# A decoder step on one core: latent attention over the cache four sequences at a time, and inter-chunk matmuls in alternating head parity

## The reference, cut to what matters

```
num = einsum('bhts,bshv->bthv', w, v) + einsum('bht,bthk,bhkv->bthv', e_inter, q, C)
```

```
s = (einsum('bthc,bsc->bhts', ql, ckv) + einsum('bthr,bsr->bhts', qr, krope)) * SOFTMAX_SCALE
s = where(k_pos[None, :] <= qp[:, None], s, -inf)
p = softmax(s, axis=-1)
o = einsum('bhts,bsc->bthc', p, ckv)
```

## Time and profile before

| what | us |
|---|---|
| median of three runs | 2011.48 (2008.69 to 2012.48) |
| profiled execution | 2009.03 |
| its span | 2007.4 |
| PE busy | 1830.7 |
| DVE busy | 1213.2 |
| ACT busy | 925.8 |
| inter-chunk matmuls, first to DVE's copy | 152.94 to 174.73 |
| sample attention, first transpose to `uv` | 732.84 to 893.67 |
| `uv` and `wo` | 893.67 to 935.4 |
| first MoE matmul | 981.59 |

### The profile page before, as it was taken

How to read it: one execution, slowest core, us unless ns; L and a number is a source line. 1 busy time by engine, 2 the same in 40 slices (tenths; PEclk the granted TensorE clock), 3 DMA queues, 4 the chain that set the end, 5 groups by cost and what they waited for, 6 DMA issues and landing times.

```text
span 2007.4 us, 23398 instructions
## 1 busy us (share of the span) xinstructions
PE 1830.7 (91%) x8410; PEld 1404.4 (70%) x8410; DVE 1213.2 (60%) x1250; ACT 925.8 (46%) x808; POOL 92.0 (5%) x155
## 2 busy tenths in 40 slices
PE   5999979999979878888799999999999999999994
PEld 4746657999954553347587787877878778787783
DVE  2102684444344332223488888888888888888886
ACT  1100022443211111102477777777777677777774
POOL 2100020001001002200100000000000000000001
PEclk9995559999989568898799999999999999999997
DMA  9910042434724002202399999999999999999993
GB/s 275 366 44 1 0 48 89 165 100 130 223 87 171 10 0 62 70 14 105 135 368 370 357 369 338 388 359 359 370 338 386 358 360 369 341 380 353 371 366 138
DMA packets 219023, 458.37 MB, mean 228 GB/s; under 512 B 11189, under 2 KB 45562, under 8 KB 218762
## 3 DMA queue, kind: packets, MB, share of 16 engines
q1 hardware_dynamic: 209034, 428.96, 59.7%
q0 software_dynamic: 8656, 28.13, 5.0%
q10 hardware_dynamic: 1280, 0.54, 0.2%
HBM read 447.11 MB, written 17.30 MB: 231 GB/s over the span
## 4 chain that ended last, share of the span: by engine, by line
PE 83%; DVE 7%; ACT 5%; issue 2%; DMA 2%; POOL 0%; SPq 0%; ACTq 0%; POOLq 0%; DVEq 0%
PE bank L388 15%; PE bank L390 15%; PE bank L389 15%; PE bank L384 8%; ACT wpart L1580 3%; PE wide L390 2%; PE wide L388 2%; PE wide L389 2%; PE bank L759 2%; DVE wpart L916 2%; PE bank L568 2%; PE wide L742 2%; PE bank L800 2%; PE bank L703 1%; PE wide L397 1%
## 5 line engine op out<-in xcount | busy, mean ns | idle before, releaser
L916 DVE TENSOR_TENSOR wpart<-mring,wpart 128x2048 fp32r<-128x2048 f32 x339 | 775.5, 2290 | 159.3 <-ACT wpart L1580 158.4
L1580 ACT ACTIVATE wpart<-mring 128x2048 fp32r<-128x2048 f32 x336 | 643.0, 1917 | 202.3 <-PE bank L390 109.1
L388 PE MATMUL bank<-wpart,xgp 128*128 128x512 f32 x896 | 360.5, 402 | 7.5 <-DVE wpart L916 5.3
L390 PE MATMUL bank<-wpart,xgp 128*128 128x512 f32 x896 | 354.4, 396 | 0.0
L389 PE MATMUL bank<-wpart,xgp 128*128 128x512 f32 x896 | 354.3, 395 | 0.0
L388 PEld LDWEIGHTS bank<-wpart,xgp 128*128 128x128 f32 x896 | 168.5, 188 | 54.4 <-DVE wpart L916 12.9
L390 PEld LDWEIGHTS bank<-wpart,xgp 128*128 128x128 f32 x896 | 168.4, 188 | 41.1
L389 PEld LDWEIGHTS bank<-wpart,xgp 128*128 128x128 f32 x896 | 168.7, 188 | 37.5
L388 PE MATMUL bank<-ffparts,wpart 128*128 128x288 f32 (+1 forms) x528 | 159.3, 302 | 5.4 <-DVE ffparts L916 4.2
L390 PE MATMUL bank<-ffparts,wpart 128*128 128x288 f32 (+1 forms) x528 | 157.4, 298 | 0.0
L389 PE MATMUL bank<-ffparts,wpart 128*128 128x288 f32 (+1 forms) x528 | 155.1, 294 | 0.0
(11 more groups left out here) (344 smaller groups left out, 2150.5 us busy)
## 6 DMA issues: line engine op xcount, KB each, us to landing
mring<-in_w_gate_m SPq DMA_DIRECT2D x114, 1024.0 KB, 5.5
mring<-in_w_up_m SPq DMA_DIRECT2D x113, 1024.0 KB, 5.7
mring<-in_w_down_m SPq DMA_DIRECT2D x112, 1024.0 KB, 5.2
ring<-in_w_in_a SPq DMA_DIRECT2D x6, 2048.0 KB, 24.0
ring<-in_w_down_d SPq DMA_DIRECT2D x8, 1344.0 KB, 7.5
ring<-in_w_gate_d SPq DMA_DIRECT2D x5, 2048.0 KB, 8.7
ring<-in_w_up_d SPq DMA_DIRECT2D x5, 2048.0 KB, 9.0
xrow<-in_zeros POOLq DMA_DIRECT2D x13, 512.0 KB, 13.5
```

The costliest lines, as they stand in the source:

```text
L388: pe.matmul(o, a[0], b[0], start=start, stop=False)
L390: return pe.matmul(o, a[0], b[1], start=False, stop=stop)
L916: return v.tensor_tensor(dst, src, high.bitcast(F32), ALU.subtract)
L1580: a.activation(wpart[:, stage(h), 0, :], mring[:, place(h % IH), :], ACT.Copy).then_inc(S["hi_ready"], 1)
```

## The change

Inter-chunk matmuls: the loop over heads becomes a loop over pairs of heads, and inside it over sequences and then over the two parities.

Sample attention: the eight sequences form two groups of four (`GROUPS`, `GB`). A sequence of a group has its 32 query rows on array columns 32t to 32t+31 and its scores and outputs on PSUM partitions 32t to 32t+31. Keys are turned in eight units of 256 tokens x 4 sequences (`turn_keys`), five bank-fulls a unit through banks 0 to 2, the rotary keys of two sequences in one transpose. Scores of a unit are twelve matmuls in the order latent part, then sequence. Scores of the 4 new tokens take one matmul a part for all four sequences. Softmax runs once a group on 128 rows; probabilities are turned in full 128 x 128 blocks through `wide`, and `s_attend` goes page by page over the four sequences.

All 64 pages are now held at once, in the arena and in ring slots 0 to 4, so that they are requested before the stage; `uv` is loaded after them and last of the ring's chunks, and chunks from the eighth on move by one slot. The seven first MoE halves are requested when the second group's `s_attend` is done. The first three splits of MoE weights move apart.

```
-            for h in range(H):
-                r, g = (h % 2) * DK, h // 2
-                o = bank[(6, 0)[h % 2] + g // 3][0:TS, (g % 3) * (DV + 1):(g % 3 + 1) * (DV + 1)]
+            for g in range(HP):
                 for b in range(NB):
-                    ins = pe.matmul(o, qbd[r:r + DK, g, b * TS:(b + 1) * TS], Ce[r:r + DK, g, b, :],
-                                    start=(b == 0), stop=(b == NB - 1))
+                    for par in range(2):
+                        r = par * DK
+                        o = bank[(6, 0)[par] + g // 3][0:TS, (g % 3) * (DV + 1):(g % 3 + 1) * (DV + 1)]
+                        ins = pe.matmul(o, qbd[r:r + DK, g, b * TS:(b + 1) * TS], Ce[r:r + DK, g, b, :],
+                                        start=(b == 0), stop=(b == NB - 1))
...
+            def turn_keys(n):
+                g, q = n // 4, n % 4
+                if q == 0:
+                    for b in range(GB * g, GB * (g + 1)):
+                        pe.wait_ge(ck_full[b], 16 * NPG)
+                    for pair in range(GB // 2 * g, GB // 2 * (g + 1)):
+                        pe.wait_ge(cr_full[pair], 32 * NPG)
+                for e in range(GB + 1):
+                    m = (GB + 1) * n + e
+                    if m >= 3:
+                        pe.wait_ge(S["tpa_free"] if (m - 3) % 2 == 0 else S["tpd_free"], (m - 3) // 2 + 1)
...
+            def s_scores(n):
...
+                for k in range(CT + 1):
+                    for t in range(GB):
+                        b = GB * g + t
+                        w, x = (qls[:, k, b, :], kc[n % 2][:, t, k, :]) if k < CT else (qrp[:, b, :], kr[n % 2][:, t // 2, :])
+                        ins = pe.matmul(wide[t * TS:(t + 1) * TS, q * QK:(q + 1) * QK], w, x, start=(k == 0), stop=(k == CT))
...
+            def turn_probs(g):
+                pe.wait_ge(S["p_exp"], NU + g + 1)
+                for pg in range(NPG):
+                    ins = pe.transpose(wide[:, pg * P:(pg + 1) * P], prob[:, pg * P:(pg + 1) * P], ident)
...
+            def s_attend(g):
...
                 for pg in range(NPG + 1):
                     rows = P if pg < NPG else TS
...
+                    for t in range(GB):
+                        x = ctk[GB * g + t][:, pg, :] if pg < NPG else ctok[0:TS, 2, 0:CKV]
+                        ins = pe.matmul(bank[3][t * TS:(t + 1) * TS, 0:CKV], PTs[0:rows, pg * P + t * TS:pg * P + (t + 1) * TS],
+                                        x, start=(pg == 0), stop=(pg == NPG))
...
+            turn_keys(0)
+            turn_keys(1)
+            for n in range(4):
+                s_scores(n)
+                turn_keys(n + 2)
+            turn_probs(0)
+            s_attend(0)
+            for n in range(4, UNITS):
+                s_scores(n)
+                if n + 2 < UNITS:
+                    turn_keys(n + 2)
+            turn_out(0)
+            turn_probs(1)
+            s_attend(1)
+            turn_out(1)
...
+            for n in range(5):
+                take_keys(n)
+            group_max(0)
+            take_keys(5)
+            take_probs(0)
+            scale_out(0)
...
+            split(0, 0)
             for m in range(DC):
                 add_residual(m)
-                if 4 <= m < 4 + STAGES:
-                    split(0, m - 4)
+                if m == 4:
+                    split(0, 1)
...
+            split(0, 2)
             v.wait_ge(S["rank_full"], 1)
...
+            a.wait_ge(S["av_full"], GROUPS)
+            first_high(0)
...
+                if name == "uv":
+                    for b in range(2, NB):
+                        sp.wait_ge(*release[CH[("dkv", "dq", "uk")[b // 2 - 1]]])
+                        load_cache(b)
...
-            under = [CH[name] for name in ("dkv", "dkv", "dq", "dq", "uk", "wo1", "wo1")]
+            sp.wait_ge(S["av_full"], GROUPS)
             for h in range(HALVES):
...
                 expert_half(0, h)
```

More of the change, by code:

```diff
@@ L242, in build @@
         S = {n: sem(n) for n in names}
[L243 to L244 removed]
+        ck_full = [sem(f"ck_full{b}") for b in range(NB)]
+        cr_full = [sem(f"cr_full{n}") for n in range(NB // 2)]
         w_full = [sem(f"w_full{k}") for k in range(SLOTS)]
@@ L713, in _ @@
             NU = len(units)
[L715 to L729, removed]
-                    ins.then_inc(S["tp_full"], 1)
@@ L746, in s_attend @@
-            def s_attend(b):
-                pe.wait_ge(S["p_exp"], NU + b + 1)
+            def turn_keys(n):
[9 more added lines that the diff above has]
+                        pe.wait_ge(S["tpa_free"] if (m - 3) % 2 == 0 else S["tpd_free"], (m - 3) // 2 + 1)
+                    for half in range(2):
+                        for pg in range(2):
+                            if e < GB:
+                                src = ctk[GB * g + e][:, 2 * q + pg, half * P:(half + 1) * P]
+                            else:
+                                src = crp[GB // 2 * g + half][:, 2 * q + pg, :, :].rearrange("p s c -> p (s c)")
+                            ins = pe.transpose(bank[m % 3][:, half * QK + pg * P:half * QK + (pg + 1) * P], src, ident)
+                    ins.then_inc(S["tp_full"], 1)
@@ L1222, in _ @@
             NU = len(units)
[L1224 to L1229, removed]
-                        ins = v.tensor_copy(cacheT[:, part, half * 512:(half + 1) * 512], bank[1][:, :])
-                    else:
-                        ins = v.tensor_copy(cacheR[:, half * 512:(half + 1) * 512], bank[1][0:ROPE, :])
-                    ins.then_inc(S["tpd_free"], 1)
@@ L1256, in _, with take_keys @@
-            turned(NB - 1)
+            def take_keys(n):
+                for e in range(GB + 1):
+                    m = (GB + 1) * n + e
+                    if m % 2:
+                        v.wait_ge(S["tp_full"], m + 1)
+                        if n >= 2:
+                            v.wait_ge(S["ks_done"], n - 1)
+                        dst = (kc[n % 2][:, e, :, :] if e < GB else kr[n % 2]).rearrange("p a k -> p (a k)")
+                        v.tensor_copy(dst, bank[m % 3][:, :]).then_inc(S["tpd_free"], 1)
@@ L1560, in _, with take_keys @@
-            for h in range(STAGES):
+            NU = len(units)
+            def take_keys(n):
+                for e in range(GB + 1):
+                    m = (GB + 1) * n + e
+                    if m % 2 == 0:
+                        a.wait_ge(S["tp_full"], m + 1)
+                        if n >= 2:
+                            a.wait_ge(S["ks_done"], n - 1)
+                        dst = (kc[n % 2][:, e, :, :] if e < GB else kr[n % 2]).rearrange("p a k -> p (a k)")
+                        a.activation(dst, bank[m % 3][:, :], ACT.Copy).then_inc(S["tpa_free"], 1)
```

238 lines of the change are left out of this document (120 added, 118 removed).

## The result

The changed kernel takes 1872.08 us (median of five runs, 1861.03 to 1874.4) against 2010.69 before (five runs): a ratio of 0.9305, 95% interval 0.9291 to 0.9319.

The account below looks back on a forecast made before the run. The prediction took PE, 83% of the chain that ended last, to bound the kernel. 2009.0 - 8.0 (inter-chunk) - 101.6 (sample attention) + 0.3 = 1899.7, with 2.45 to the median 1902 us; range 1882 to 1932.

Parts of the forecast that it names:

- Inter-chunk matmuls: Inter-chunk stretch: alternating 64-row halves overlap, 64 steps of 0.215 us take 13.8 us in place of 21.8, a gain of 8.0.
- this case: Inter-chunk stretch: both halves at work bring the clock to its upper level at once, 6.9 us, 14.9 better.
- Sample attention: First key transpose to uv: 47.2 us PE work, 7.0 waits, 5.0 clock; 59.2 in place of 160.8, gain 101.6.
- the dip: Sample attention after the second softmax: a low-clock stretch doubles the output's 3.9 us and costs 1.1 around it, 5.0 together.
- Four abreast: Sample attention's scores and outputs: four sequences' 32-column tiles run at once, 10.3 us for scores and 7.7 for outputs.
- What is hidden: Page loads, MoE halves, splits and rotary writes stay under other work; only 0.3 us is added for rotary writes and small copies.
- a loop that took longer: MoE loop, unchanged in its text: if it took longer than before, the forecast would be wrong as a whole.
- Page loads, splits, rotary writes: Pages out by 690 us, before sample attention; third split in DVE's 4.49 us wait; rotary writes about 0.18 us a head.
- Rival 1: Sample attention: strict program order lets only two tiles run abreast, 10.3 + 7.7 us more, 1920 us; chance 0.15.
- rival 3: Sample attention: 32-column tiles take turns, scores 31.0 us more and outputs 23.2, 1956 us; chance 0.06.
- Rival 2: Sample attention: lower clock throughout because transposes do not raise or hold it, 28 us more, 1930 us; chance 0.08.
- Rival 4: Sample attention: every column-tile change drains the array, 123 us more, 2025 us, slower than before; chance 0.02.

Follow-up runs that it names:

- e4: Changed kernel with sample attention's score and output matmuls ordered one sequence's steps after the other's, so neighbours share 32 columns: 1907.6 us, ratio 0.9489.
- e9: Changed kernel with thirty-two unused columns (128 bytes) ahead of xgp and hhp: 1889.29 us (four runs), ratio 0.9385.
- e7: Changed kernel with eight unused columns (32 bytes) ahead of xgp and hhp: 1886.29 us (one run).
- e8: Changed kernel with sixteen unused columns (64 bytes) ahead of xgp and hhp: 1882.62 us (one run).
- e3: Kernel before with only the inter-chunk matmuls' edit, sample attention one sequence at a time as before: 1995.39 us against 2009.7, ratio 0.9921.
- first trace: Profiled execution of the changed kernel's first measurement, nothing edited, the quickest of its five runs: 1861.03 us.
- e11: Changed kernel with eight unused columns between xgp and hhp, so that only hhp moves by 32 bytes: 1879.26 us (one run).
- e2: Kernel before once more, nothing edited: 2006.85 us.
- e6: Kernel before with eight unused columns (32 bytes) ahead of xgp and hhp: 1988.92 us, ratio 0.989.
- e18: Changed kernel, unedited, run again on one chip beside a version with a moved arena: 1871.25 us, ratio 0.9307.
- e1: Changed kernel once more, nothing edited: 1871.04 us (four runs, 1860.73 to 1873.14).

## Why the prediction was wrong

- **Inter-chunk matmuls: mis-sized, 8.0 for 14.3.** The mechanism held: pairs side by side, 0.215 us a step. The step that failed was to stay at 13.8 us "because ... the clock stands at 0.50 for all of these 22 us". That clock was the one of one half at work at a time. With both at work it rose 3.4 us into the stretch, and the matmuls went on at 0.11: the 21.8 us up to DVE's copy became 9.0. The rest of the 14.3 lies behind the copy, where the clock stayed at 1.00 to 166.80 and had been at 0.50. The forecast had named this case, with a gain of 14.9, and set it aside.
- **Sample attention: right, 59.2 forecast and 54.88 measured.** PE waits 54.88 - 48.33 = 6.55 us (forecast 7.0). 160 transposes at 2.46 / 20 = 0.123 are 19.7 (21.8); eight units of scores at 1.43 are 11.4 (10.3 and a share of the 1.5 for changes); the outputs 4.22 + 6.29 = 10.5 (11.6, the dip included). The dip was mis-sized: it cost 2.1 in the output, not 3.9, because the clock rose before its end. Four abreast, which no row of before had shown, held, and e4 shows that it rests on the order: the same matmuls in the other order made the stage 33 us longer.
- **What is hidden: the loop was left out as unchanged.** This is the step that put the time outside the range. The text of the loop did not change, but the addresses of its operands did: the diff's line on `smask` widens the constants table by four columns, and the forecast has no word on the shift of what is allocated behind it. It was worth 8 x 2.38 = 19.0 us by the traces, the largest part of the 30 between 1902 and 1872; the two stages above gave 6.3 and 4.3 more than forecast. It is luck: nothing in the change aimed at it. e9, the changed kernel without that luck, took 1889.29 (four runs), e7 and e8 1886.29 and 1882.62 (one each), all inside the range. The forecast warned of a loop that took longer; it had no case for one that took less.
- **Page loads, splits, rotary writes:** PE waited for none of them; nothing to correct.
- **The rivals** fell. Rival 1 asked for 2.6 us a unit and rival 3 for 5.2; it was 1.43. Rival 2 asked for the lower clock throughout: it was 0.91 on the mean. Rival 4 would have been slower than before.

The sum: 14.3 (e3) + 105.9 (160.8 - 54.88) + 19.0 - 1.4 = 137.8 of the 138.6 us measured between the medians. The terms come from single traces, and e3's gain alone lies anywhere from 12 to 19 us, so an agreement to a microsecond is partly chance. The two profiled executions lie 148.0 us apart; the 10 beyond the sum are the shorter prompt attention of the first trace, 79.4 us for 89.1.

## What to carry to other kernels

Read a diff for what it allocates as well as for what it runs: a table four columns wider moved a stage of half the run by 2%. If a loop is bound by PE, compare the start-to-start step of its matmuls before and after, even where its text is the same, and try the places of its two operands against each other with a few unused columns. When matmuls use a part of the array, let neighbours in the program go to different parts, and look at the granted clock as well: in the inter-chunk stretch here it rose with that order.

## What the runs showed of the hardware

- A matmul of 512 float32r columns with 128 x 128 stationary takes 0.227 us (median) from start to start where its stationary and its streamed operand lie at the same place modulo 256 bytes, and 0.232 to 0.234 at distances of 32, 64, 128 and 224; e11 has both in one loop. That is a finding on five distances. Why, the traces do not show: weight loads take 187 to 188 ns in both. The Trainium skill, "SBUF — State Buffer", section "Operand start alignment", asks of an operand's start only that it be a multiple of the element size, and says that this is about legality, not speed. Every place here is such a multiple, and the paces differ by 2 to 3%.
- In the dense feed-forward, with operands in the other roles and 288 columns, distance 0 is not the best: 133.3 ns, against 132.2 at 64 and 224 and 134.0 at 32. So there is no one rule on distances here; the place has to be tried.
- 64-row matmuls that keep one half of the array busy at a time ran at 0.50 for the whole 22 us of the stretch in all three traces of that order (before, e2, e6). With the two halves in turn the clock was at 1.00 from 2.9 to 4.5 us after the first of them on, in all sixteen traces of that order (3.4 in the first).
- PE starts matmuls for another tile past a few that are still to start (three between two heads; e4's scores, 2.80 us for 5.2). In e4's outputs, 18 for one tile in a row with the last two of another shape, nothing overlapped (16.53 us).
- The changed kernel, unedited, kept prompt attention at the lower clock for 47.8, 58.0 or 81.9 us in different executions (first trace, e18, e1), 79.4 to 89.8 us for the stage. What decides it stays open.
